# Page steps of a paged-attention stage in a new order: full-array work, then scores and values, with one buffer of turned keys and a fifth page slot

## The reference

```python
k_past = cache_k[a, page_table].reshape(b_s, past_len, N_HEADS, 2, HEAD_DIM)
v_past = cache_v[a, page_table].reshape(b_s, past_len, N_HEADS, V_DIM)
o_s = diff_attend(qs, pos_new, ((k_past, v_past, pos_past), (kn, vn, pos_new)), lam, slopes)
```

## Time and profile before

| | |
|---|---|
| runs | 3186.69, 3187.70 (median), 3192.26 us |
| profiled execution | 3186.87 us |
| its span (first to last instruction) | 3185.1 us |
| mean granted clock of PE | 0.995 of full speed |
| busy: PE, PEld | 3103.1 us (97%), 2913.4 us (91%) |
| busy: DVE, ACT, POOL | 1507.0 us (47%), 1065.2 us (33%), 278.3 us (9%) |
| DMA over the span | 637.98 MB, 200 GB/s |

### The profile page before, as it was taken

The page is one execution under the profiler, slowest core; times in us unless marked ns, Lnnn a source line. Parts: engine busy times, 40 slices in busy tenths (PEclk is TensorE's granted clock), DMA queues, the critical chain, the costliest instruction groups (busy, mean ns, idle before and its releaser), DMA issues.

```text
span 3185.1 us, 59411 instructions
## 1 busy us (share of the span) xinstructions
PE 3103.1 (97%) x25406; PEld 2913.4 (91%) x25406; DVE 1507.0 (47%) x2160; ACT 1065.2 (33%) x1502; POOL 278.3 (9%) x226
## 2 busy tenths in 40 slices
PE   8999999999988899999999999999999999999998
PEld 8987877787766699999999999999999999999998
DVE  4344444444444454444444444447544444445445
ACT  3233333333333433223222323225333233233333
POOL 0022222222210010000000000004000000000002
PEclk9999999999999999999999999999999999999999
DMA  6469999999998545444444444443444444444442
GB/s 199 147 237 366 362 353 359 373 359 359 361 331 310 193 140 167 137 147 141 146 142 137 144 147 134 146 146 102 145 144 148 152 149 150 148 155 148 146 152 94
DMA packets 341938, 637.98 MB, mean 200 GB/s; under 512 B 11528, under 2 KB 257775, under 8 KB 308367
## 3 DMA queue, kind: packets, MB, share of 16 engines
q1 hardware_dynamic: 337120, 620.67, 55.9%
q0 software_dynamic: 3328, 11.24, 1.0%
q10 hardware_dynamic: 1230, 2.29, 0.2%
HBM read 625.37 MB, written 9.23 MB: 199 GB/s over the span
## 4 chain that ended last, share of the span: by engine, by line
PE 88%; DVE 5%; ACT 3%; issue 2%; DMA 2%; SPq 0%; POOL 0%; ACTq 0%; DVEq 0%; POOLq 0%
PE ps L1688 71%; PE ps L1804 7%; PE ps L1852 3%; PE ps L1829 3%; DVE halves L1121 1%; ACT halves L815 1%; DMA raw<-in_cache_k_dram 1%; PE ps L1957 1%; DVE pa_n L1414 1%; PE ps L1937 1%; PE ps L2100 0%; DVE pa_s L1408 0%; ACT pa_s L953 0%; DMA io_tm<-in_x_sample_dram 0%; PE ps L1842 0%
## 5 line engine op out<-in xcount | busy, mean ns | idle before, releaser
L1121 DVE TENSOR_TENSOR halves<-raw,halves 128x2048 fp32r<-128x2048 f32 x300 | 687.9, 2293 | 667.3 <-ACT halves L815 667.2
L1688 PE MATMUL ps<-xhi,halves 128*128 128x320 f32 (+1 forms) x3840 | 861.7, 311 | 4.6 <-DVE halves L1121 2.4
L815 ACT ACTIVATE halves<-raw 128x2048 fp32r<-128x2048 f32 x300 | 573.4, 1911 | 867.9 <-PE ps L1688 860.8
L1688 PE MATMUL ps<-yhi,halves 128*128 128x336 f32 x2816 | 657.2, 318 | 0.1
L1688 PEld LDWEIGHTS ps<-xhi,halves 128*128 128x128 f32 x3840 | 649.9, 188 | 6.0 <-issue 4.8
L1688 PE MATMUL ps<-xlo,halves 128*128 128x320 f32 (+1 forms) x1920 | 598.2, 312 | 0.0
L1688 PEld LDWEIGHTS ps<-yhi,halves 128*128 128x128 f32 x2816 | 483.1, 188 | 0.5 <-issue 0.4
L1688 PE MATMUL ps<-ylo,halves 128*128 128x336 f32 x1408 | 447.2, 318 | 0.0
L1308 DVE TENSOR_SCALAR keyT<-ps 128x512 f32<-128x512 f32 x256 | 177.0, 692 | 463.4 <-PE ps L1804 463.4
L1688 PE MATMUL ps<-hA_hi,halves 128*128 128x336 f32 (+1 forms) x1408 | 375.6, 314 | 2.9 <-DVE hT L1579 2.8
L1688 PE MATMUL ps<-hB_hi,halves 128*128 128x336 f32 (+1 forms) x1408 | 372.8, 312 | 0.0
(11 more groups left out here) (224 smaller groups left out, 3076.0 us busy)
## 6 DMA issues: line engine op xcount, KB each, us to landing
raw<-in_w_gate_up_dram SPq DMA_DIRECT2D x176, 1024.0 KB, 5.1
raw<-in_cache_k_dram SPq DMA_DIRECT2D x124, 1024.0 KB, 6.8
raw<-in_cache_v_dram SPq DMA_DIRECT2D x121, 1024.0 KB, 8.3
raw<-in_w_down_dram SPq DMA_DIRECT2D x88, 1024.0 KB, 5.0
kv_raw<-in_w_qkv_dram SPq DMA_DIRECT2D x64, 512.0 KB, 8.4
raw<-in_w_qkv_dram SPq DMA_DIRECT2D x16, 1024.0 KB, 5.1
raw<-in_w_o_dram SPq DMA_DIRECT2D x16, 1024.0 KB, 5.4
page<-in_cache_v_dram SPq DMA_DIRECT2D x7, 1024.0 KB, 7.2
```

Of the source, the lines that this page charges most:

```text
L815: act.activation(whi[t][:, :], raw[r][:, :], ACT.Copy).then_inc(hi_ready[t], 1)
L1121: dve.tensor_tensor(wlo[t][:, :], raw[r][:, :], whi[t][:, :].bitcast(F32), ALU.subtract)\
L1688: mm = pe.matmul(out, l, r, start=first and n == 0, stop=last and n == 2)
```

## The change

Each engine's loop is written in a new order. The loop now starts at t = 0 and turns and scores the same page in one step. On PE a step does first what uses the array with 128 columns (key transposes, projection, tiles, probability transposes) and then, at its end, scores and values (32 columns). The first chunk of projection lies between the two halves of the transposes, the second behind them. In a step of `KV_END` the block is turned in the first chunk's place, and both chunks follow the second half.

There is one buffer `keyT`; the copies into it wait for the scores of the step before. In the second buffer's place lies a fifth page slot. ACT and DVE take their copies in the order that belongs to this. The probabilities of the last four pages are turned together, into four parts of one bank, and their values follow in the last step. The new-token steps and the pairs come one and two steps earlier, and a new token's probabilities are turned into PSUM bank 4. The row loads of the residual are spread over steps 113 to 118 in POOL's program. What each product computes is as before.

The diff, cut to its core:

```diff
 PAGES = NB * NPAGE
-SLOTS = 6
+SLOTS = 7
...
 TURN_LAG, VALUE_LAG = 5, 6
-STEPS = PAGES + VALUE_LAG
+STEPS = PAGES + 2
+def turned_in(t):
+    first = [v for v in (t - TURN_LAG,) if 0 <= v < PAGES - GROUP]
+    return first + (list(range(PAGES - GROUP, PAGES)) if t == STEPS - 1 else [])
+def valued_in(t):
+    if t < PAGES:
+        return [v for v in (t - VALUE_LAG,) if v >= 0]
+    return [PAGES - VALUE_LAG, PAGES - VALUE_LAG + 1] if t == PAGES else list(range(PAGES - GROUP, PAGES))
...
 NEW_SEQ = (7, 0, 1, 2, 3, 4, 5, 6)
-NEW_AT = {114 + n: n for n in range(NB)}
-PAIR_AT = {124 + 2 * p: p for p in range(3)}
-HX0 = 124
+NEW_AT = {113 + n: n for n in range(NB)}
+PAIR_AT = {122 + 2 * p: p for p in range(3)}
+HX0 = 122
+BACK_AT = (113, 114, 115, 116, 118)
...
 def page_order():
-    order = [("k", n) for n in range(4)] + [("w", n) for n in range(3, 11)]
+    order = [("k", n) for n in range(4)] + [("w", n) for n in range(3, 11)] + [("k", 4)]
     for t in range(STEPS):
-        if 4 <= t + 1 < PAGES:
-            order.append(("k", t + 1))
-        if 0 <= t - VALUE_LAG:
-            order.append(("v", t - VALUE_LAG))
+        if 5 <= t < PAGES:
+            order.append(("k", t))
+        order.extend(("v", v) for v in valued_in(t))
...
 def page_slots():
-    last, turns, out = {i: None for i in range(4)}, {i: 0 for i in range(SLOTS)}, []
+    last, turns, out = {i: None for i in range(5)}, {i: 0 for i in range(SLOTS)}, []
...
         if n == MORE_FROM:
-            last.update({4: None, 5: None})
+            last.update({5: None, 6: None})
...
         sp.wait_ge(split_ready[half_slot], half_turn + 1)
+    elif slot == RAW:
+        sp.wait_ge(unit_used[1], 9)
...
     act.wait_ge(kt_full, 4 * t + g + 1)
-    if t >= 2:
-        act.wait_ge(s_full, t - 1)
-    act.activation(keyT[t % 2][:, 512 * g:512 * g + 512], ps[g % 2][:, :], ACT.Copy)\
+    if t:
+        act.wait_ge(s_full, t)
+    act.activation(keyT[:, 512 * g:512 * g + 512], ps[g % 2][:, :], ACT.Copy)\
...
 def probs_out(v):
-    act.wait_ge(pt_full, v + 1)
+    act.wait_ge(pt_full, v + 1 if v < PAGES - GROUP else PAGES)
...
         act.wait_ge(v_done, v - 3)
-    src = ps[2][:, 2 * P:3 * P].rearrange("p (m a x) -> p a m x", a=2, x=2 * NT)
+    at = probs_at(v)
+    src = ps[2][:, at:at + P].rearrange("p (m a x) -> p a m x", a=2, x=2 * NT)
...
         act.wait_ge(nv_done, n)
-    src = ps[2][0:ROWS[2], 3 * P:4 * P].rearrange("p (m a x) -> p a m x", a=2, x=2 * NT)
+    src = ps[4][0:ROWS[2], P:2 * P].rearrange("p (m a x) -> p a m x", a=2, x=2 * NT)
...
 act.wait_ge(cleared, 5)
-for t in range(-1, STEPS):
-    if t + 1 < PAGES:
-        keys_out(t + 1, 0)
+for t in range(STEPS):
+    if t < PAGES:
+        keys_out(t, 0)
+    if t - 1 in NEW_AT:
+        new_exps(NEW_AT[t - 1])
+    if t in KV_END:
+        kv_rows(KV_END[t])
...
         tile_squares(tile_at(t, 4))
-    if t + 1 < PAGES:
-        keys_out(t + 1, 2)
-    if t in KV_END:
-        kv_rows(KV_END[t])
-    for n in range(9, 4 * KV_BLOCKS):
-        if KV_FIRST[n - 1] == t:
-            kv_split_hi(n)
+    if t < PAGES:
+        keys_out(t, 2)
...
         tile_features(tile_at(t, 5))
+    for v in turned_in(t):
+        if v < PAGES - GROUP:
+            probs_out(v)
+    if t - 1 in NEW_AT:
+        new_probs_out(NEW_AT[t - 1])
+    for n in range(9, 4 * KV_BLOCKS):
+        if KV_FIRST[n - 1] == t:
+            kv_split_hi(n)
...
         exps(t // GROUP - 1)
-    if 0 <= t - TURN_LAG < PAGES:
-        probs_out(t - TURN_LAG)
-    if t - 1 in NEW_AT:
-        new_exps(NEW_AT[t - 1])
-        new_probs_out(NEW_AT[t - 1])
+    for v in turned_in(t):
+        if v >= PAGES - GROUP:
+            probs_out(v)
...
 dve.wait_ge(cleared, 5)
-for t in range(-1, STEPS):
-    if t + 1 < PAGES:
-        keys_out(t + 1, 1)
+for t in range(STEPS):
+    if t in KV_END:
+        kv_features(KV_END[t])
+    if t < PAGES:
+        keys_out(t, 1)
+    if t in NEW_AT:
+        if NEW_AT[t]:
+            dve.wait_ge(n_full, NEW_AT[t])
+        queries(NEW_SEQ[NEW_AT[t]], 2, qn_set)
+    if t in KV_END:
+        kv_rows(KV_END[t])
...
         tile_normed(tile_at(t, 5))
-    if t in KV_END:
-        kv_features(KV_END[t])
...
         out_means(PAIR_AT[t - 1])
-    if t + 1 < PAGES:
-        keys_out(t + 1, 3)
-    if 0 <= t < PAGES:
-        scores_out(t)
-    if t in KV_END:
-        kv_rows(KV_END[t])
-    if 0 <= t < PAGES and t % GROUP == GROUP - 1:
-        maxima(t // GROUP)
+    if t < PAGES:
+        keys_out(t, 3)
+    if t - 1 in NEW_AT:
+        new_sums(NEW_AT[t - 1])
...
         tile_join(tile_at(t, 2))
+    if t in PAIR_AT:
+        factors(PAIR_AT[t])
...
         back_features(2 * (t - HX0) + 1)
-    if t - VALUE_LAG >= 0 and (t - VALUE_LAG) % GROUP == GROUP - 1:
-        add_values((t - VALUE_LAG) // GROUP)
...
         dve.wait_ge(padded, 8)
-    if t + 1 in NEW_AT:
-        if NEW_AT[t + 1]:
-            dve.wait_ge(n_full, NEW_AT[t + 1])
-        queries(NEW_SEQ[NEW_AT[t + 1]], 2, qn_set)
-    if t - 2 in NEW_AT:
-        new_values(NEW_AT[t - 2])
+    if t < PAGES:
+        scores_out(t)
+    if t < PAGES and t % GROUP == GROUP - 1:
+        maxima(t // GROUP)
...
         new_scores_out(NEW_AT[t])
+    for v in valued_in(t):
+        if v % GROUP == GROUP - 1:
+            add_values(v // GROUP)
     if t - 1 in NEW_AT:
-        new_sums(NEW_AT[t - 1])
-    if t in PAIR_AT:
-        factors(PAIR_AT[t])
+        new_values(NEW_AT[t - 1])
...
         pe.wait_ge(s_out, t)
-    if t - TURN_LAG > 0:
-        pe.wait_ge(pt_out, t - TURN_LAG)
-    turned = sum(at + 1 < t for at in NEW_AT)
-    if turned:
-        pe.wait_ge(nt_out, turned)
+    if 0 <= t - TURN_LAG < PAGES - GROUP:
+        pe.wait_ge(pt_out, t - TURN_LAG + 1)
...
         mm = pe.matmul(ps[2][32 * b:32 * b + 32, 0:PAGE], qp[i % 2][:, at:at + 32],
-                       keyT[t % 2][:, P * j:P * j + P], start=(a == 0), stop=(a == 3),
+                       keyT[:, P * j:P * j + P], start=(a == 0), stop=(a == 3),
...
     mm.then_inc(pa_back, 1)
-for t in range(-1, STEPS):
-    if t + 1 < PAGES:
-        turn_keys(t + 1, 0)
-    if 0 <= t < PAGES:
-        scores(t)
+for t in range(STEPS):
+    work = list(KV_AT.get(t, ()))
+    if t < PAGES:
+        turn_keys(t, 0)
+    if t in KV_END:
+        turn_block(KV_END[t])
+    elif work:
+        project(*work.pop(0))
+    if tile_at(t, 5) is not None:
+        tile_back(tile_at(t, 5))
...
         tile_turn(tile_at(t, 3))
-    if tile_at(t, 5) is not None:
-        tile_back(tile_at(t, 5))
...
         turn_back(2 * (t - HX0))
-    if t + 1 < PAGES:
-        turn_keys(t + 1, 1)
-    if t in KV_END:
-        turn_block(KV_END[t])
-    if t - VALUE_LAG >= 0:
-        values(t - VALUE_LAG)
-    if t - 2 in NEW_AT:
-        new_values(NEW_AT[t - 2])
-    for block, cc in KV_AT.get(t, ()):
-        project(block, cc)
-    if 0 <= t - TURN_LAG < PAGES:
-        turn_probs(t - TURN_LAG)
+    if t < PAGES:
+        turn_keys(t, 1)
+    for v in turned_in(t):
+        if v < PAGES - GROUP:
+            turn_probs(v)
...
         turn_new_probs(NEW_AT[t - 1])
-    if t in NEW_AT:
-        new_scores(NEW_AT[t])
-    if HX0 <= t < HX0 + 8:
-        turn_back(2 * (t - HX0) + 1)
...
         tile_values(tile_at(t, 3))
+    if HX0 <= t < HX0 + 8:
+        turn_back(2 * (t - HX0) + 1)
+    for block, cc in work:
+        project(block, cc)
+    if t < PAGES:
+        scores(t)
+    for v in turned_in(t):
+        if v >= PAGES - GROUP:
+            turn_probs(v)
+    for v in valued_in(t):
+        values(v)
+    if t - 1 in NEW_AT:
+        new_values(NEW_AT[t - 1])
+    if t in NEW_AT:
+        new_scores(NEW_AT[t])
```

More of the change, by code:

```diff
@@ L313, in trunk @@
         aT_new = place("aT_new", [P, 2, 144], F32, hT_at)
-        pages = raw + [place(f"page{i}", [P, UNIT], F32, x_at + 3 * D * 4 + i * UNIT * 4) for i in range(2)]
+        late = [place(f"page{5 + i}", [P, UNIT], F32, x_at + 3 * D * 4 + i * UNIT * 4) for i in range(2)]
         assert 3 * D * 4 + 2 * UNIT * 4 <= 2 * DC * T * 4
@@ L324, in trunk @@
         aT = [place(f"aT{i}", [P, 2, 144], F32, z + i * 288 * 4) for i in range(4)]; z += 4 * 288 * 4
-        keyT1 = place("keyT1", [P, UNIT], F32, z); z += UNIT * 4
+        page4 = place("page4", [P, UNIT], F32, z); z += UNIT * 4
         assert z <= halves_at + SPLIT * 2 * UNIT * 4
+        pages = raw + [page4] + late
         z = b_at
-        keyT = [place("keyT0", [P, UNIT], F32, z), keyT1]; z += UNIT * 4
+        keyT = place("keyT", [P, UNIT], F32, z); z += UNIT * 4
         sc = [place(f"sc{i}", [P, GROUP * PAGE], F32, z + i * GROUP * PAGE * 4) for i in range(3)]
@@ L549, in tile_at, with probs_at @@
             return None
+        def probs_at(v):
+            return 2 * P if v < PAGES - GROUP else P * (v % GROUP)
         def nth(n, ring, i=0, step=0):
@@ L718, in kv_split_lo, with row_back @@
                                    kv_hi[n % KV_HI][:, :].bitcast(F32), ALU.subtract).then_inc(kv_split, 1)
```

(34 more changed lines are left out.)

11 lines of the change are left out of this document (2 added, 9 removed).

## The result

The changed kernel takes 3199.25 us (median of 20 runs, 3187.36 to 3206.63), the kernel before in the same comparison 3188.77 (20 runs, 3186.58 to 3192.95). The ratio is 1.0027, with a 95% interval of 1.0019 to 1.0034: a little slower. The forecast was 3174 with 3150 to 3196, so the time is outside the range and on the other side. The runs of the changed kernel fall into two groups: six from 3187.4 to 3191.5 at a mean granted clock of 0.995 or 0.996, and fourteen from 3197.4 to 3206.6 at 0.991 to 0.993. The profiled execution is one of the fourteen (3200.41 us, span 3198.6); the profiled execution before has a span of 3185.1.

What follows compares the result with a forecast made beforehand. PE was taken to set the pace, with DMA nearly full at 97%. From the profiled 3186.9 us, -3.6 in the steady part, -2.4 in new-token steps and -7 for key pages gave 3174 us, range 3150 to 3196.

Steps and rivals of the forecast that it cites:

- The steps with projection: Steady part of the attention stage over seven heads: switch savings, removed waits and new waits together give -3.6 us.
- the old waits go: Steps with projection: PE's waits for copied keys (8.6 us) and normed tiles (3.1) taken off, 11.7 us.
- The switches: PE's changes between 128- and 32-column work, four to two per step: 0.30 us saved in each of 106 steps, 31.8 us.
- The listed waits: New PE waits for tile weights, turned features, tile norms and finished blocks: 5.7 us per head, +39.9 over seven heads.
- One buffer of keys: Scores need the same step's key copies; the second projection chunk covers them with 0.10 us to spare: cost 0.
- rival B: VectorE's fourth key copy comes late in plain steps, scores stand 0.25 us in 106 steps: +26, 3200 us; chance 0.20.
- The last stretch with its new tokens and pages: Attention stage after the projections: -2.4 us in new-token steps and -7 around key-page waits, -9.4 predicted.
- the fifth slot: Extra key-page buffer lets loads go half a step (3 us) earlier, taking 6 of 9.0 us of page waits off.
- Rival C: The tail is paced by its transfers, so shorter steps only wait longer and it gives nothing: 3183 us; chance 0.15.
- The end: End of the attention stage, last group and pairs: short steps and hand-overs go, yet 0 us, bounds -4 and +4.
- the same stage waits: Reason for expecting 0 at the attention stage's end: waits (5.5 us) still stand between values and joining of pairs.
- The floor of the transfers: At 365 GB/s and 97% busy, a 16-step period needs no less than 103.6 us, 3.2 less than now.

Runs made afterwards that it cites:

- the kernel with all moves: Changed kernel with tile exponentials behind the next key copy, tile work behind cover, block features early, pairs at the step's end: 3124.89 us, 0.9803 of the kernel before.

## Why the prediction was wrong

- **The steps with projection: -3.6 forecast, +11.4 measured.** The failing step is "the old waits go". Its 11.7 us were taken off as "re-made in new places below", but no place below held ScalarE's key copy: the list had tile weights, features, norms and blocks. A wait for that copy was there again, 10.7 us, with some 0.16 of overlap for each of its 14 times 13 us. Without it a period is 106.49, and -0.5 us a period had been forecast (106.3). I had looked for waits that the new PE order makes and not at ScalarE's own order, in which the exponentials of one step stand directly before the first copy of the next. The change leaves that order as it was, so there was no reason to strike the wait out.
- **The switches were right for a plain step:** 5.74 us, 0.34 saved where 0.30 was forecast. Over all steps they were worth less, by an estimate: the kernel with all moves hardly waits and takes 695.4 us from the scores of page 0 to those of page 112, 44.8 less than before. The old waits make 18.4 of that (11.7 idle and 0.16 for each of 42 times), which leaves some 26 for the switches, where 31.8 was forecast.
- **That the rest of the sum came out is partly luck.** The old waits were taken off at 11.7, their idle time alone, and the new ones put in with their overlap; the 6.7 missing there nearly cancel the 5 too many for the switches. So the steps without the omitted wait come to -1.3, near the -3.6.
- **The listed waits were right,** each of them. Idle time plus 0.16 for each time: weights 7.9 + 3.4 = 11.3 (forecast 7 x 1.7 = 11.9), features 6.7 (6.3), norms 13.2 (14.7), blocks 6.1 + 2.1 = 8.2 (7): 39.4 against 39.9. That the order itself makes them, and that cover takes them away, is shown by the run with the tiles moved.
- **One buffer of keys (rival B) was priced rightly at nothing** where a projection covers it: no wait of the scores for VectorE's copy in the steps with projection, 3.8 us in the last stretch where no projection is left. The time came out near B's 3200, but not by B.
- **The last stretch with its new tokens and pages: right as a sum** (-9.9 against -9.4), and in part by luck. Its parts were not right: the fifth slot gave 3 us, where the forecast gave the slot all of its 6, yet all waits for pages went. PE's busy time, with more of it at full clock, gave 3.2, where the forecast had 1 for the clock. Rival C is refuted, since the stretch gave 9.9 us and not nothing.
- **The end: +2.3, inside its bounds of -4 and +4,** but "the same stage waits" was not a reason: turning out a pair waits 4.5 us where it waited 1.1, since both stand now right behind what feeds them. The lower clock adds to it. The runs show that 11 us could be had there.
- **The floor of the transfers (103.6 us) was no floor.** I read 97% busy as capacity. The same bytes went through in 100.4 us. Here a share of 0.95 to 0.97 at 357 to 365 GB/s did not tell that more could not be carried. The Trainium skill's figure of about 358 GB/s for one core (DMA: Bandwidth & Descriptors, Specifications) is exceeded further: 386 GB/s over a period.
- **After the stage: 0 forecast, +10.4 in the profiled execution.** The clock in the pooling layer was no term at all. No row of the stage could have shown it, and the mean clock of 0.995 did not point there: in the trace before, half clock stands in the last stretch of the attention stage (0.95 over 145 us), behind it (0.50 from 1065 to 1075 us) and at the end of the program. That this loss fell on top was bad luck for the forecast. The runs that kept the clock are at 3187 to 3191, inside the range, but the forecast of a gain fails there too: no change against before, as the steps' loss and the last stretch's gain cancel.

## What to carry to other kernels

When work is moved away from what covered a wait, list the waits of every engine in its new order, and let a wait that is struck out name the place in the code where its cause has gone; a wait "re-made below" has to be found below. Put a small operation at least one block of long work behind what feeds it: here four such moves turned a change of 0.3% to the worse into 2% to the better. Compare two kernels stage by stage before whole times: here 1.9 us of added work could lose 10 in a place that nobody touched.

## What was not expected of the hardware

- **A two-column VectorE operation stands while POOL works.** In 14 of 14 cases L1445 lasted until 0.02 to 0.03 us after POOL's subtraction, 1.39 us in the rows shown, and it took 0.17 where POOL did not work; moving it to ScalarE removed 10.3 us of PE's waits. The Trainium skill, SBUF — State Buffer, section on SBUF's two separate sides, states that VectorE and GpSimd share a port pair which one of them holds for a whole instruction; the trace agrees, and which kind of lock it was is not shown here.
- **The same idle time loses the clock or keeps it.** The same two gaps of 0.56 and 2.09 us are followed by half clock for about 14 us (kernel before with 1.9 us added) or 20 us (changed kernel), or by none (kernel before; the same with 3.2 us added, in its profile). In the changed kernel 14 of 20 runs show the lower mean clock.
- **A wait costs more than its idle time,** by about 0.16 us here, since the matmul behind a wait does not start within the record of the one ahead of it (0.11 us behind its start, where the record takes 0.27). Ten waits of 4.2 us idle were worth 6.1.
